# Holding the first expert's weight loads, from its fifth unit on, until the first token gather has landed

## The reference

```python
h2 = _rms_norm(x, p['norm2_g']) * (1 + sc2) + sh2
x = x + g2 * _expert_choice_ffn(h2, p)
...
def _expert_choice_ffn(h, p):            # cap = 2 * S // 16: 64 latent rows, 16 prompt rows
    logits = (h @ p['w_router']).astype(jnp.float32) + p['b_router'].astype(jnp.float32)
    aff = jax.nn.softmax(logits, axis=-1)
    gate, idx = lax.top_k(aff.transpose(0, 2, 1), cap)
    xs = jax.vmap(lambda hb, ib: hb[ib])(h, idx)
    gg = jnp.einsum('becd,edf->becf', xs, p['w_e_gate'])
    uu = jnp.einsum('becd,edf->becf', xs, p['w_e_up'])
    y = jnp.einsum('becf,efd->becd', jax.nn.silu(gg) * uu, p['w_e_down']) * gate[..., None].astype(h.dtype)
    return jax.vmap(lambda yb, ib: jnp.zeros((S, D), yb.dtype).at[ib.reshape(-1)].add(yb.reshape(-1, D)))(y, idx)
```

## Time and profile before

| | |
|---|---|
| three runs | 1319.16, 1322.58, 1323.9 us (median 1322.58) |
| the profiled execution | 1323.25 us, its span 1321.4 us |
| PE busy | 1221.4 us (92%) |
| DVE, ACT, POOL busy | 909.2, 618.1, 313.9 us |
| bytes by DMA | 302.89 MB, 229 GB/s over the span |
| SP's queue | 145636 packets, 272.80 MB |
| chain that ended last | PE 86%, DVE 6%, DMA 2%, ACT 2%, POOL 2% |

### The profile page before, as it was taken

How to read it: one execution, slowest core, us unless ns; L and a number is a source line. 1 busy time by engine, 2 the same in 40 slices (tenths; PEclk the granted TensorE clock), 3 DMA queues, 4 the chain that set the end, 5 groups by cost and what they waited for, 6 DMA issues and landing times.

```text
span 1321.4 us, 18915 instructions
## 1 busy us (share of the span) xinstructions
PE 1221.4 (92%) x7370; PEld 988.9 (75%) x7370; DVE 909.2 (69%) x1021; ACT 618.1 (47%) x688; POOL 313.9 (24%) x209
## 2 busy tenths in 40 slices
PE   5899889999999999997997199999999999999995
PEld 3788669998999999997997166666666666666663
DVE  3599766445553325324656779999999999999996
ACT  4311222224442124132213177777777777777774
POOL 1041100001442232233224302222222222222225
PEclk9899989999999889999998599999999999999998
DMA  9876641312111111235206989999999999999985
GB/s 322 258 203 211 197 88 64 112 65 73 49 49 64 64 56 62 76 143 176 67 10 249 383 317 357 380 380 380 381 381 381 381 382 381 381 382 385 382 318 179
DMA packets 156264, 302.89 MB, mean 229 GB/s; under 512 B 7058, under 2 KB 60821, under 8 KB 155952
## 3 DMA queue, kind: packets, MB, share of 16 engines
q1 hardware_dynamic: 145636, 272.80, 57.7%
q0 software_dynamic: 3872, 12.78, 4.1%
q10 hardware_dynamic: 6700, 16.51, 3.4%
HBM read 286.98 MB, written 15.08 MB: 229 GB/s over the span
## 4 chain that ended last, share of the span: by engine, by line
PE 86%; DVE 6%; DMA 2%; ACT 2%; POOL 2%; issue 1%; ACTq 0%; SPq 0%; POOLq 0%; DVEq 0%
PE bank L1496 17%; PE bank L1497 16%; PE bank L1498 16%; PE bank L1520 5%; PE bank L1522 5%; PE bank L1521 5%; PE bank L1525 5%; PE bank L1524 5%; PE bank L1523 5%; PE bank L1748 2%; DVE fa L1060 1%; PE bank L1552 1%; DMA xg_f<-in_x_sample 1%; PE bank L1733 1%; DMA g2r<-scratch_mods 1%
## 5 line engine op out<-in xcount | busy, mean ns | idle before, releaser
L894 ACT CAST h2r_a<-w_a 128x2048 fp32r<-128x2048 f32 x96 | 183.8, 1914 | 79.3 <-PE bank L1498 77.1
L1496 PE MATMUL bank<-h2r_a,xTh 128*80 128x512 f32 x384 | 152.4, 397 | 1.4 <-DVE xTl L1415 1.4
L561 POOL TENSOR_TENSOR half<-half 1x1 f32<-1x1 f32 x33 | 69.9, 2118 | 348.7 <-DVE ye L1463 345.8
L1498 PE MATMUL bank<-h2r_a,xTl 128*80 128x512 f32 x384 | 150.5, 392 | 0.0
L489 POOL TENSOR_TENSOR lring<-wring,hring 128x2048 fp32r<-128x2048 f32 x21 | 98.9, 4711 | 190.7 <-ACT hring L629 190.7
L1497 PE MATMUL bank<-l2r_b,xTh 128*80 128x512 f32 x320 | 125.7, 393 | 0.0
L1409 DVE TENSOR_TENSOR l2r_b<-w_a,h2r_b 128x2048 fp32r<-128x2048 f32 x48 | 110.3, 2299 | 17.8 <-ACT h2r_b L894 17.8
L1409 DVE TENSOR_TENSOR l2r_a<-w_a,h2r_a 128x2048 fp32r<-128x2048 f32 x48 | 109.6, 2283 | 12.6 <-ACT h2r_a L894 7.7
L1409 DVE TENSOR_TENSOR l2r_b<-w_a,h2r_a 128x2048 fp32r<-128x2048 f32 x48 | 109.9, 2289 | 10.2 <-ACT h2r_a L894 10.2
L1060 DVE SCALAR_TENSOR_TENSOR fa<-fa,cwT 128x655 f32<-128x655 f32 x120 | 111.5, 972 | 1.4
L894 ACT CAST h2r_b<-w_a 128x2048 fp32r<-128x2048 f32 x48 | 91.9, 1915 | 34.7 <-PE bank L1498 31.9
(11 more groups left out here) (333 smaller groups left out, 3061.6 us busy)
## 6 DMA issues: line engine op xcount, KB each, us to landing
w_a<-in_w_e_gate SPq DMA_DIRECT2D x64, 1024.0 KB, 12.8
w_a<-in_w_e_up SPq DMA_DIRECT2D x64, 1024.0 KB, 13.8
w_b<-in_w_e_down SPq DMA_DIRECT2D x48, 1024.0 KB, 12.5
wring<-in_w_in SPq DMA_DIRECT2D x20, 1024.0 KB, 5.2
w_a<-in_w_e_down SPq DMA_DIRECT2D x16, 1024.0 KB, 13.4
fa<-in_w_ada SPq DMA_DIRECT2D x14, 1024.0 KB, 7.9
wring<-in_w_ada SPq DMA_DIRECT2D x10, 1024.0 KB, 9.5
fa<-in_w_in SPq DMA_DIRECT2D x4, 1024.0 KB, 11.3
```

Source lines behind the costliest of these rows:

```text
L894: act.copy(h2r[k % 3], w2[k]).then_inc(e_hi, 1)
L1496: pe.matmul(out, lh, rh, start=start, stop=False)
L1498: return pe.matmul(out, ll, rh, start=False, stop=stop)
```

## The change

SP, in the first expert alone, waits before the load of unit 4 until the first gather has landed (`e_x` at 16). The loads of units 0 to 3 are issued as before.

```diff
                     elif k == 2:
                         unit_used(sp, N_U - 1)
+                    elif k == 4:
+                        sp.wait_ge(e_x, 16)
                     elif k == 9:
                         sp.wait_ge(s_hst[3], 16)
```

## The result

The changed kernel took 1333.56 us in the median of four runs (1330.63 to 1335.93), the kernel before 1320.87 us in four runs (the three of the table above and one more): ratio 1.0095, 95% interval 1.0079 to 1.0112. That is 0.95% slower, outside the range (1319 to 1328) and past the 0.5% to which the prediction gave 0.09. The same kernel in a later comparison (e10): 1331.18 against 1321.51 us, ratio 1.0080 (1.0066 to 1.0095).

A forecast was written before the change was run, and what follows sets the result against it. PE was taken to bound the kernel (busy 92% of the span), with DMA queues nearly as tight. The terms -3.2 at the start and +3.6 at the end gave +0.4: 1323.0 us forecast, range 1319 to 1328.

The forecast's parts named there:

- the gain: Between routing and first expert: no DVE wait for g2r, sooner gather, first matmul at about 752.6 instead of 755.82, -3.2 us.
- The debt: Expert stage after the first expert: 0.56 us lost per expert, 14 experts take 7.8 us from a lead of about 8.
- rival 3: Expert stage: the lead runs out experts before the end, PE goes at the DMA's pace, 1329.2 us or more; chance 0.09.
- the first expert: covered: First expert's weight loads: units 4 and 11 land before ACT wants them, lead 7 to 8 us, no stall.
- slower by over 0.5%: Same as rival 3: decided by a rate from 376.6 GB/s on or a gather releasing SP at 755; chance 0.09.
- the last term: Last expert: fin lands behind the last weights and delays ACT's casts of units 10 and 11, +3.6 us.

The follow-up runs named there:

- e10: The changed kernel measured again in a later comparison: 1331.18 us against 1321.51 us for the kernel before, ratio 1.0080.
- e3: The kernel before, loading only half of unit 11 from the second expert on (output differs): 1321.30 us, ratio 1.0004 to the kernel before.
- e7: The kernel before with ACT's first two squares of the last expert moved behind the cast of unit 11: 1322.17 us, ratio 1.0008.
- e8: The changed kernel with DVE's first low part held until the first gather has landed: one run, 1328.07 us.
- e9: The kernel before with loads held from unit 8, DVE waiting for POOL's first gather issue, token parts before the third low part: 1318.18 us, ratio 0.9980.
- e2: The changed kernel, loading only half of unit 11 from the second expert on (output differs): 1318.51 us, ratio 0.9985 to the kernel before.
- e5: The changed kernel with the wait at unit 8 instead of unit 4: 1319.16 us, ratio 0.9978 to the kernel before.
- e1: The changed kernel with ACT's first two squares of the last expert behind the cast of unit 11: 1327.15 us, ratio 1.0042 to the kernel before.
- e11: The changed kernel with the wait at unit 6 instead of unit 4: 1326.42 us, ratio 1.0040 to the kernel before.
- e6: The changed kernel with loads held until PE has finished unit 0 of the first expert: 1335.66 us, ratio 1.0107 to the kernel before.

## Why the prediction was wrong, point by point

**Right.** The place and the mechanism of the gain: DVE's wait for `g2r` went, and the gather came sooner. The debt, and that nothing refills the lead. That `fin` lands behind the last weights and holds ACT in order ahead of unit 10: forecast as a stall of 4.2 us (1290.3 to 1294.5), measured 5.4. The pace of the DMA, 34.75 us an expert forecast, 34.84 measured. Of the signs that were named for a wrong forecast, the one of rival 3 came: PE idle for DMA before the last expert.

**The step that failed first is "the first expert: covered".** It put the lead in the first expert at 7 to 8 us, from the sum of bytes in front of a unit and 0.7 us for completion, and looked at units 4 and 11 alone. For the landing of unit 4, alone on idle queues, that was exact (after 5.1 us). The tightest unit was unit 7. Its issue by SP, its time to landing in the list of DMA issues, and its cast by ACT:

```profile
749.88 0.69 SPq L455 DMA_DIRECT2D w_a<-in_w_e_up  x1
w_a<-in_w_e_up SPq DMA_DIRECT2D x1, 1024.0 KB, 14.9
766.43 1.91 ACT L896 CAST h2r_a<-w_a 128x2048 fp32r<-128x2048 f32 x1 [0.85 <-PE bank L1500]
```

It landed at 764.8, and the lead was 1.7 us. The sum erred on both sides. Unit 11 was to land 24.6 us after the gather and to be wanted 32.8 after it; it landed 26.7 us after it (issued at 756.72, landed 18.3 us later) and was cast after 30.6. So its lead was 3.9 us and not 8.2.

The loads were late because here a load in a full queue shared the bandwidth with those behind it. Unit 9 was issued at 753.74 and landed 16.2 us later, at 769.9. Six units and the second gather, 6.6 MB, at the 378 GB/s of that stretch, are through 17.5 us after the 750.0 at which bytes began to flow, and with 0.7 us for completion would have landed at 768.2. In that list for 750.0 to 769.9, SP's queue stands with (packets, MB, share):

```profile
q1 hardware_dynamic: 2848, 7.10, 96.6%
```

Units 4 to 9 are 6.29 MB. The other 0.8 MB, 2.1 us at that rate, went to loads issued behind unit 9. The casts were early for two reasons. The first matmul came 2.4 us after the gather's landing and not 3.7. And the casts then followed it 0.9 us faster than in the profile of before (unit 11 after 28.2 us instead of 29.1), whose clock rose later: from 4.2 to 6.2 us after the first matmul the granted clock was 0.69 there and 1.00 here. That is no effect of the change, since in e3 and e7, which have no hold, unit 11 was cast after 28.2 and 28.1 us.

From the second expert on unit 10 was the tightest. It landed 3.1 us before its cast there (24.1 in the kernel before), 1.8 in the third and 0.6 in the fifth expert; in the sixth ACT waited for it. From there PE went at the pace of the DMA: +4.9 us where the sum had nothing. The last load of weights landed at 1297.6 (issued at 1278.49, landed 19.1 us later), where the forecast had its last byte at 1291.7. The rival "slower by over 0.5%" named this, but I let it be decided by a lower rate or a late gather, and neither was needed. The rate was 380 instead of 381 GB/s.

**The second is the size of the last term**: +3.6 us forecast, +7.6 measured. The stall was 1.2 us longer. `fin` was issued 7.8 us after the scatter-add (1282.14 to 1289.90) and its first tile landed 9.0 us later, against 5.3 and 5.2 before: 6.2 us, less 0.7 of slack. The other 2.9 us are TensorE's clock after the stall, which the sum left out: after 4.56 us of standing still the granted clock was 0.50 for 5.6 us. The Trainium skill (TensorE: Matmul & The Clock Gate, section on what's actually happening) says that the throttled state is the default and that activity releases it. This trace agrees, and I did not use it.

**The third is the gain**: -3.2 us forecast, -2.2 measured. DVE was not the later side. The gather landed in 5.8 us rather than 3.5, and the first matmul followed 2.4 us later: 8.2 us in all, where 7.2 were forecast, set by DVE. Of the 5.8 us, 1.8 are POOL's issue beside DVE's low parts, a coupling that the removed wait had hidden. On idle queues and with DVE still it takes 3.9 to 4.1 us (e8, e9), against 7.6 in the kernel before. So contention cost this gather 3.5 us. The Trainium skill's rule on turns between queues (DMA: Bandwidth & Descriptors, section on queues, rings and completion order), from which the prediction had estimated about 0.9 us, was too mild a guide here. These parts make the difference: +1.0, +4.9 and +4.0 on a forecast of +0.4 are the measured +10.3.

**Shown and not shown.** Shown: the loss is work put off (e2 against e3, e5), the stall at the square and the pace of the DMA are two losses (e1, e11, e8), and the squares' place is harmless without the debt (e7). That bandwidth went to the loads behind unit 9 is read from the bytes moved in one trace; no run changed it alone. The price of the clock after the stall is read from the rows, and not tested apart from the stall. Open: why the longer hold of e6 cost less than its length.

## What to carry to other kernels

In this expert stage PE and its DMA are within 2% of each other (34.19 and 34.84 us an expert). In such a stage the time that the queues idle ahead of it is a debt, to be compared with the lead. Read the lead from landing times in a full queue against the use of the tightest unit, for every unit, and not from bytes over rate for two of them. To clear the way for a small urgent transfer, hold only as many loads as the lead can repay: holding four units gained 2 us, six lost 5, eight lost 10 to 13. Look at what else stands in the same queue and is waited for in order at the end, and price a stall of TensorE with its clock.

## What the runs showed of the hardware that I had not expected

POOL's issue of the first indirect gather took 2.91 us beside DVE's float32 subtractions and 1.07 us without them (e8, e9), and in e8 the second gather took 2.83 when it came beside them. In the expert loop the issue beside them is 0.97 us, while POOL's one-element add before it takes 4.3 us instead of 0.18. In e8 the same add took 2.12 us when it came beside the low parts. So in these rows POOL is held up for about 2 to 4 us beside DVE's subtractions, in whichever operation it has; for the adds of the expert loop no run took DVE's work away. The Trainium skill (DMA: Bandwidth & Descriptors, section SWDGE vs HWDGE vs iDMA) says that DVE locks GpSimd out of SBUF during two-port modes; these runs show a delay of the issue beside a plain `tensor_tensor`, and cannot tell whether that is the same lock.
